# Attention gate products cut into quarter pieces among the attention jobs, and scores that no longer wait for their bias

## What is computed

```python
proj = h @ w_in                       # q, k, v, index parts, z, xbc, dt, g_attn, g_ssd
a = dsa_attention(q, k, v, q_idx, k_idx, w_idx)   # 8 heads of 128, 2 kv heads, causal, top 64 of the keys
b = mamba2_branch(...)
merged = sigmoid(g_attn) * (a @ w_proj_attn) + sigmoid(g_ssd) * (b @ w_proj_ssd)
x = x + merged @ w_out                # then a gated feed-forward part
```

## Time and profile before

| | |
|---|---|
| median of 3 runs | 3262.22 us (3258.53 to 3264.95) |
| profiled execution | 3261.8 us, of which span 3260.0 us |
| mean granted TensorE clock | 0.951 of full speed |
| PE busy | 2927.1 us (90% of the span) |
| DVE, ACT, POOL busy | 1055.1, 579.5, 200.1 us |
| DMA | 720.06 MB, mean 221 GB/s |

### The profile page before, as it was taken

One profiled execution on the slowest core, in us unless ns is written; L12 is line 12 of the kernel. 1 busy time (PEld: TensorE's weight loads), 2 busy tenths in 40 slices (PEclk: granted clock), 3 DMA queues, 4 the chain that ended last, 5 costly groups with the idle time before them and its releaser, 6 DMA issues. The chain is left out here.

```text
span 3260.0 us, 34241 instructions
## 1 busy us (share of the span) xinstructions
PE 2927.1 (90%) x13990; PEld 1738.8 (53%) x13990; DVE 1055.1 (32%) x2733; ACT 579.5 (18%) x1276; POOL 200.1 (6%) x367
## 2 busy tenths in 40 slices
PE   7899999999899998999999799999929987888984
PEld 4476557854476555865576555445414554333331
DVE  3443333423433433522454422122141243111112
ACT  1322311101321311101252100000000231000000
POOL 0000040000000000000000000000020020000001
PEclk9999999999999999999999799999959998999997
DMA  6255356344245446642211199999953224999995
GB/s 228 71 187 207 129 172 243 129 146 155 79 153 215 146 144 219 207 151 78 87 69 61 41 415 428 428 427 427 420 186 107 82 66 168 428 427 428 421 428 233
DMA packets 183270, 720.06 MB, mean 221 GB/s; under 512 B 16032, under 2 KB 25216, under 8 KB 158016
## 3 DMA queue, kind: packets, MB, share of 16 engines
q1 hardware_dynamic: 163600, 667.51, 52.3%
q0 software_dynamic: 19216, 50.24, 4.8%
q10 hardware_dynamic: 288, 0.01, 0.0%
HBM read 694.02 MB, written 25.53 MB: 221 GB/s over the span
## 5 line engine op out<-in xcount | busy, mean ns | idle before, releaser
L2329 PE MATMUL bank<-wslot,xgT 128*64 128x512 f32 x1040 | 479.6, 616 | 81.5 <-DMA wslot<-in_moe_w_up 72.9
L517 PE MATMUL bank<-h1T,wslot 128*128 128x256 f32 x2176 | 481.0, 383 | 0.0
L2330 PE MATMUL bank<-wslot,xgT 128*64 128x512 f32 x1040 | 480.3, 617 | 0.0
L517 PEld LDWEIGHTS bank<-h1T,wslot 128*128 128x128 f32 x2176 | 416.7, 192 | 59.4 <-issue 2.1
L2329 PEld LDWEIGHTS bank<-wslot,xgT 128*64 128x64 f32 x1040 | 142.6, 142 | 356.8 <-issue 356.8
L2346 DVE TENSOR_TENSOR hid<-gs,bank 64x512 f32<-64x512 f32 x65 | 67.7, 1042 | 527.7 <-ACT gs L2340 527.7
L2384 PE MATMUL bank<-wslot,aT 128*64 128x512 f32 x1040 | 230.3, 595 | 1.5 <-DVE aT L591 1.5
L2304 PE MATMUL bank<-sel,hT 128*128 128x128 f32 x1600 | 191.2, 280 | 20.4 <-DVE sel L2283 20.4
L2304 PEld LDWEIGHTS bank<-sel,hT 128*128 128x128 f32 x1600 | 184.9, 195 | 45.8 <-issue 25.2
L2330 PEld LDWEIGHTS bank<-wslot,xgT 128*64 128x64 f32 x1040 | 142.5, 142 | 16.4 <-issue 16.4
L2384 PEld LDWEIGHTS bank<-wslot,aT 128*64 128x64 f32 x1040 | 72.8, 137 | 135.3 <-issue 131.8
(11 more groups left out here) (374 smaller groups left out, 3492.2 us busy)
## 6 DMA issues: line engine op xcount, KB each, us to landing
wslot<-in_moe_w_gate SPq DMA_DIRECT2D x65, 2048.0 KB, 16.8
wslot<-in_moe_w_up SPq DMA_DIRECT2D x65, 2048.0 KB, 12.4
wslot<-in_moe_w_down SPq DMA_DIRECT2D x65, 2048.0 KB, 13.8
wslot<-in_w_in SPq DMA_DIRECT2D x36, 2048.0 KB, 8.7
wslot<-in_w_ada SPq DMA_DIRECT2D x24, 2048.0 KB, 8.1
wslot<-in_ffn_w_up SPq DMA_DIRECT2D x20, 2048.0 KB, 9.2
y_rows<-yo POOLq DMA_DIRECT2D x130, 128.0 KB, 7.7
wslot<-in_w_proj_ssd SPq DMA_DIRECT2D x8, 2048.0 KB, 7.8
```

The source lines that it names most:

```text
L517: ins = pe.matmul(b.t[:, 0:width], w[:, k, j * P:(j + 1) * P], xT(k), start=(k == 0), stop=(k == kc - 1))
L2329: pe.matmul(bk.t[other, :], xt.t[:, k, mine], wg[:, k, :], start=(k == 0), stop=(k == KD - 1))
L2330: ins = pe.matmul(bk.t[mine, :], xt.t[:, k, mine], wu[:, k, :], start=(k == 0), stop=(k == KD - 1))
```

## The change

The gate products are emitted in pieces of two of the eight contraction steps by a new generator `tokens_pieces`; a tile takes four pieces, and the pipeline emits one piece in each round (16 pieces, 16 jobs). All pieces go into one bank that is taken out of the turn of eight until the jobs are done. ACT copies the raw result to `gate`; after the jobs two sigmoids, each over a whole row of 1024 columns, run in place. No gate tile is emitted ahead of the flush any more. `attend` has a new argument `biased`: marks for which only DVE waits, ahead of the bias add, and no longer PE ahead of the score product. The first block passes the mask's mark so, the neighbourhood attention the mark of the added window. The joint attention passes nothing.

```diff
--- before.py
+++ after.py
@@ -446,6 +446,27 @@
             bank.free = [use(t, bank.t[:, 0:n], self.mt)]
             yield
 
+    def tokens_pieces(self, key, xT, n_tiles, deps, use, bank, per):
+
+
+        i, w, landed = self.take(key)
+        kc, n = w.shape[1], w.shape[2]
+        for t in range(n_tiles):
+            for k0 in range(0, kc, per):
+                @self.block.tensor
+                def _(pe):
+                    for due in self.due(pe, landed, *deps, *(bank.free if k0 == 0 else ())):
+                        pe.wait_ge(*due)
+                    for k in range(k0, k0 + per):
+                        ins = pe.matmul(bank.t[:, 0:n], xT(k, t), w[:, k, :], start=(k == 0), stop=(k == kc - 1))
+                    if k0 + per == kc:
+                        self.mt = self.pe.mark(ins.then_inc(self.pe.sem, 1))
+                if k0 + per == kc:
+                    if t == n_tiles - 1:
+                        self.give(i, self.mt)
+                    bank.free = [use(t, bank.t[:, 0:n], self.mt)]
+                yield
+
     def tokens_out(self, tiles, xT, n_tiles, deps, use, cols=None):
 
 
@@ -639,7 +660,7 @@
         a.free = b.free = [self.mr]
         return self.mr
 
-    def attend(self, w, q, k, values, nk, bias, first, put, deps):
+    def attend(self, w, q, k, values, nk, bias, first, put, deps, biased=()):
 
 
         b = self.banks.next()
@@ -659,7 +680,7 @@
 
         @self.block.vector
         def _(v):
-            for due in self.due(v, ready, *stfree, *deps):
+            for due in self.due(v, ready, *stfree, *deps, *biased):
                 v.wait_ge(*due)
             if bias is not None:
                 for due in self.due(v, self.dve.mark(v.tensor_tensor(b.t[:, first:nk], b.t[:, first:nk], bias, ALU.add)
@@ -1009,22 +1030,14 @@
         gm = {}
 
         def use_gate(n):
-            def use(t, bank, mk):
-                @block.scalar
-                def _(act):
-                    for due in K.due(act, mk):
-                        act.wait_ge(*due)
-                    K.mg = K.act.mark(act.activation(gate[:, t, 512 * n:512 * n + 512], bank, ACT.Sigmoid).then_inc(K.act.sem, 1))
-                gm[n, t] = K.mg
-                return K.mg
-            return use
+            return lambda t, bank, mk: K.copy(1, gate[:, t, 512 * n:512 * n + 512], bank, mk)
+        held = K.banks.bufs.pop()
 
         def gates():
 
             for n in range(2):
-                yield from K.tokens_steps(("ga", l, n), xT, TT, hdeps, use_gate(n))
+                yield from K.tokens_pieces(("ga", l, n), xT, TT, hdeps, use_gate(n), held, 2)
         beside = gates()
-        next(beside)
         K.flush()
         for t in range(TT):
             @block.vector
@@ -1045,13 +1058,20 @@
                 g = h // (HEADS // KVH)
                 jobs.append(K.attend(w, qT[:, h, t * P:(t + 1) * P], kT[:, g, 0:nk],
                                      [vt[:, i, g * HD:(g + 1) * HD] for i in range(t + 1)], nk,
-                                     score[:, t, 0:nk], 0, rows, [last[t], *ready]))
-        pipeline(jobs, 7, beside, 5)
+                                     score[:, t, 0:nk], 0, rows, ready, [last[t]]))
+        pipeline(jobs, 7, beside)
+        K.banks.bufs.append(held)
+        for t in range(TT):
+            @block.scalar
+            def _(act):
+                for due in K.due(act, (K.act, K.act.count)):
+                    act.wait_ge(*due)
+                gm[t] = K.act.mark(act.activation(gate[:, t, :], gate[:, t, :], ACT.Sigmoid).then_inc(K.act.sem, 1))
         for n in range(2):
             def use(t, bank, mk):
                 @block.vector
                 def _(v):
-                    for due in K.due(v, mk, gm[n, t]):
+                    for due in K.due(v, mk, gm[t]):
                         v.wait_ge(*due)
                     K.mg = K.dve.mark(v.tensor_tensor(acc[:, t, 512 * n:512 * n + 512], bank,
                                                       gate[:, t, 512 * n:512 * n + 512], ALU.mult).then_inc(K.dve.sem, 1))
@@ -2236,7 +2256,7 @@
             b, added = fetched[n]
             yield from K.attend(w, qT[:, h, t * P:(t + 1) * P], kT[:, h // 2, :],
                                 [vn[:, k, h * HD2:(h + 1) * HD2] for k in range(NT2)], 512, b.t[:, i, t, :], SEQ,
-                                rows[t], [*ready, *added])
+                                rows[t], ready, added)
             if t == TT - 1 and i == 3:
                 b.free = [(K.dve, K.dve.count)]
                 if n + 2 < HC // 4:
```

## The result

The changed kernel takes 3237.67 us (median of 4 runs, 3235.5 to 3249.0) beside 3260.52 us of the kernel before: a ratio of 0.9933, with an interval of 0.9912 to 0.9954, so some 22 us faster. The forecast was 3235 with a range of 3228 to 3247. A second set of runs gave 3236.82 us against 3259.80, again 0.9933 (0.9919 to 0.9947). The profiled execution is the slowest of the first four, 3249.0 us; why is told further down.

What follows compares the result with a forecast made beforehand. TensorE was taken to bound the first block. Attention stages 10.4 and 9.5, neighbourhood waits 5.7 and clock 4.6, less 3.2 for gaps, gave 27.0 us off 3261.8: 3234.8, called 3235, range 3228 to 3247.

Steps and rivals of the forecast that it cites:

- What bounds: First block: TensorE is busy nearly everywhere, DMA share 0.48 between attention stages, so only time taken from TensorE counts.
- rival C: Whole kernel: saved time is waited for at weights or in the expert stages, leaving 3262 us; chance 3%.
- The start: First attention stage: kv transposes wait for the rope, a new gap of 2.9 us replacing the old 1.90.
- the masks' wait: First score product, first block: 2.89 us wait goes, covered by pieces while DVE finishes masks; without cover it returns.
- Pieces, jobs, held bank, seams: Attention stage on PE: 16 pieces 27.4 us, jobs 11.3, stalls on the one held bank 0.8, piece boundaries 0.8.
- The tail: Attention stage, last score product's end to projection: 6.4 us instead of 7.35, as DVE has no gate-tile backlog.
- The stage: First block attention: projection at 142.2 instead of 152.63, gaining 10.4 us in layer 0 and 9.5 in layer 1.
- Sigmoids: End of attention stage: two sigmoids and a table load hide under the first projection tile; without that cover 3.3 us.
- Neighbourhood: Neighbourhood attention: two stalls shrink by 2.85 us each, 5.7 together, and low-clock losses of 2.9 and 1.7 go too.
- A gap of this size costs 0 or 1.6: Clock after each of four remaining gaps near 3 us: loss 0 or 1.6, charged 0.8 each, 3.2 in all.
- Sum: Whole kernel: 10.4 + 9.5 + 5.7 + 4.6 - 3.2 = 27.0 us faster, forecast 3235 us.
- Rival D: Attention stages: small pieces and bank turns make the clock fall, up to +27 us net, 3289 us; chance 4%.

Runs made afterwards that it cites:

- the start covered: Changed kernel with two gate pieces ahead of the flush and first-block scores waiting on PE for the mask: 3230.95 us, ratio 0.9910 to the kernel before.
- masks on PE: Kernel before with the change in the first block only, its scores still waiting on PE for the mask: 3240.93 us, ratio 0.9943.

## Why the prediction was right, step by step

- **What bounds**: held. All that left PE's queue in these stages left the span, apart from the clock elsewhere; rival C (absorbed) didn't happen, and the DMA share between the stages is 0.48 as before.
- **The start**: a gap of 2.9 us was forecast, 2.82 measured. That the masks' wait would cost 2.89 us without its cover was the wrong size: taken back alone it cost nothing in the length of the stage (in layer 1 it showed, as 1.17 us), with the start covered 1.4 us a layer.
- **Pieces, jobs, held bank, seams**: idle times of 0.35 and 0.23 us are left, which from start to start, as the forecast counts, are 0.52, 0.40 and 0.08 for the three new tiles: 1.0 instead of 0.8; seams are 0, not 0.8. The tail from the last score product's end to the projection was put at 6.4 us; from 136.92 + 0.44 to 143.91 it is 6.6.
- **The stage**: I had the projection at 142.2, it came at 143.91, with the stage begun 0.4 us late and 1.7 us lost to the clock, of which 0.8 was charged apart; the seams (-0.8), the stalls (+0.2) and the tail (+0.2) make up the rest. Gains of 9.6 and 8.7 with that charge became 9.1 and 8.3.
- **Sigmoids**: hidden. The table loads of the stage are two where there were seven.
- **Neighbourhood**: this is the term that was mis-sized. The run-ahead was right: three rounds, then a wait of 3.03 and 2.95 us for the exp, forecast as 3.1. But I took back the low clock behind the old gaps (2.9 + 1.7 us) and charged only 0.8 for each new gap. From the resumption at 2612.28 to the score product at 2618.90 the work is two value products, two transposes and a score product, 3.4 us at full pitch, and it took 6.6: a loss of 3.2 us, more than the 2.9 behind the gap of 5.78, and 3.2 again behind the second gap. So the part is worth 3.8 us by the first trace, not 8.7: 5.5 from the waits, less 1.8 for the clock. In the second trace, where the first gap cost 1.7, it is 5.2. "A gap of this size costs 0 or 1.6" was read from two gaps, both followed by nothing but large matmuls; four gaps of the changed kernel cost 1.5 to 3.2 in its two traces, and none cost 0.
- **Sum**: 27.0 forecast; 9.1 + 8.3 + 3.8 = 21.2 by the stages of the first trace and 22.8 by those of the second, 22.9 and 23.0 by the two pairs of medians. 3235 against 3237.67, inside the range, with the neighbourhood term 3.5 to 5 us too large. The spans of the two traces are 12.8 and 22.6 us under that of the kernel before, since the clock in the unchanged stretches cost more in the first one.
- **Rival D** (slower by the clock) fell: from 101.2 to 143.9 the granted clock was 1.00, with PE busy 40.38 of the 42.70 us. The rule of the Trainium skill cited there, page "TensorE: Matmul & The Clock Gate", section "A second HAM failure mode: psum-queue depth-cycling", isn't borne out in these rounds: the granted clock is 0.97 in the window of the stage, and what is missing lies behind the one gap of 2.82 us. PE was hardly idle between the groups here, so a stage with more small idle times isn't tested by it.

## What to carry to other kernels

Work put beside a latency-bound pipeline should be cut as finely as the rounds: a boundary whose waits are met cost nothing measurable, while whole tiles cost 4.4 and 5.8 us in the two stages, some 4.2 of it without the clock. The likely reason, read from the rows and not tested by itself, is that the steps of the jobs stand still behind a whole tile in PE's queue. When a cover is moved, look at what it covered: two of the sixteen pieces put back ahead of the flush gave some 7 us in the two stages. And ask of a wait not only who stands in it but when its resource is really free: the buffer's release was five rounds late, and its cure was worth more than moving the wait to another engine.

## What the runs showed of the hardware

The clock after a gap. Behind gaps of 2.8 to 3.0 us the clock fell in each of the four places of the changed kernel's first trace. The loss was 1.7 us in both attention stages, where large matmuls follow, and 3.2 us at both places of the neighbourhood stage, where small products and transposes do. That the kind of work makes the difference isn't shown: in the second trace the same work behind the same gap of 3.0 us lost 1.7 at the first of these places and 3.2 at the second. The Trainium skill's page "TensorE: Matmul & The Clock Gate", section "Why this matters for your kernels", warns of idle gaps between bursts of matmuls, behind which the clock is low; these four places agree, and the first of the earlier trace rows is a gap of 2.81 us without a fall. Of the fourteen gaps of 2.82 or 2.83 us at the start of the attention stages, in the seven traces that have them, the clock fell behind thirteen; it stayed up only in layer 1 of the version with the masks on PE.

It also falls without such a gap. In the second layer's state-space stage the same 32 matmuls behind the same gap took, in the changed kernel and in the version with the masks on PE:

```profile
1068.20 6.30 PE L1375 MATMUL bank<-xdt,decay 128*128 128x64 f32 x32 [1.63 <-DVE decay L1363]
```

```profile
1060.40 3.79 PE L1375 MATMUL bank<-xdt,decay 128*128 128x64 f32 x32 [1.62 <-DVE decay L1363]
```

From the layer 1 projection to the neighbourhood stage it is 1697.46 us in the first trace of the changed kernel, 1691.91 in its second, 1687.84 in the kernel before and 1684.22 with the masks on PE, though nothing there was changed. The spans of the two traces of the changed kernel are 9.8 us apart (3247.2 and 3237.4). Of that 5.6 lie in this stretch, 1.5 in the neighbourhood stage, and 2.4 ahead of the first attention stage, where the same 16 matmuls some 17 us into the span took 9.01 us in the one and 7.11 in the other. What set the untraced runs apart isn't known, but a spread of this kind is why whole times here can't tell 2 us apart. In the state-space stage shown the clock fell in six of the fourteen traces, both of the changed kernel among them; whether a version brings it about, by where its stages come to lie in time, or chance does, stays open.
